# The start of a fused decoder layer: which queue brings x, in which pieces the first weights are split, and fewer filler products

## The reference

```python
z = h @ w_in[l]          # h is x: (256, 2048); w_in: (2048, 1024 + 512 + 512 + 64 + 4096)
u_ssm, c_q, c_kv, k_rope_raw, gate_logits = jnp.split(z, split_at, axis=-1)
```

## Time and profile before

| | |
|---|---|
| time, median of 3 runs | 1333.01 us (1332.86 to 1333.1) |
| profiled execution | 1332.76 us, of which the span from first to last instruction is 1330.6 us |
| PE busy | 1320.0 us, 99% of the span |
| DVE busy, ACT busy | 835.4 us (63%), 648.7 us (49%) |
| transfers | 253.21 MB, mean 190 GB/s |

### The profile page before, as it was taken

The page is one execution under the profiler, slowest core; times in us unless marked ns, Lnnn a source line. Parts: engine busy times, 40 slices in busy tenths (PEclk is TensorE's granted clock), DMA queues, the critical chain, the costliest instruction groups (busy, mean ns, idle before and its releaser), DMA issues.

```text
span 1330.6 us, 28260 instructions
## 1 busy us (share of the span) xinstructions
PE 1320.0 (99%) x11052; PEld 1249.1 (94%) x11052; DVE 835.4 (63%) x1232; ACT 648.7 (49%) x910; POOL 23.1 (2%) x50
## 2 busy tenths in 40 slices
PE   9999999999999999999999999999999999999998
PEld 8999999999999998879999999999999998888896
DVE  6787868687786776577555655555555555545545
ACT  5566556474656454365444444444444453434332
POOL 0022000000001000000000000000000000000000
PEclk9999999999999999999999999999999999999999
DMA  8656545545476775754656666666666676556562
GB/s 287 206 190 191 161 157 159 154 141 183 135 192 184 250 246 197 241 169 149 200 190 190 191 195 194 191 190 197 195 190 192 215 236 193 191 173 216 175 207 98
DMA packets 79774, 253.21 MB, mean 190 GB/s; under 512 B 16544, under 2 KB 17504, under 8 KB 79584
## 3 DMA queue, kind: packets, MB, share of 16 engines
q1 hardware_dynamic: 78304, 251.69, 59.8%
q0 software_dynamic: 1408, 0.63, 0.2%
HBM read 248.08 MB, written 2.10 MB: 188 GB/s over the span
## 4 chain that ended last, share of the span: by engine, by line
PE 96%; DVE 2%; ACT 1%; DMA 1%; issue 0%; SPq 0%; DVEq 0%
PE ps L895 22%; PE ps L896 22%; PE ps L897 22%; PE ps L907 9%; PE ps L908 9%; PE ps L909 9%; PE ps L1103 1%; DVE wlo L477 1%; PE ps L1122 1%; PE ps L1099 1%; DMA xrow<-x 0%; PE ps L1034 0%; PE ps L1075 0%; PE ps L1048 0%; PE ps L1056 0%; DVE sqsum L1484 0%
## 5 line engine op out<-in xcount | busy, mean ns | idle before, releaser
L477 DVE TENSOR_TENSOR wlo<-raw,whi 128x1024 fp32r<-128x1024 f32 x450 | 546.8, 1223 | 334.1 <-ACT whi L521 332.1
L521 ACT ACTIVATE whi<-raw 128x1024 fp32r<-128x1024 f32 x450 | 476.6, 1061 | 543.0 <-PE ps L897 340.1
L895 PE MATMUL ps<-hT,whi 128*128 128x256 f32 x1376 | 378.4, 275 | 0.0
L896 PE MATMUL ps<-hT,whi 128*128 128x256 f32 x1376 | 378.4, 275 | 0.0
L897 PE MATMUL ps<-hT,wlo 128*128 128x256 f32 x1376 | 378.4, 275 | 0.0
L895 PEld LDWEIGHTS ps<-hT,whi 128*128 128x128 f32 x1376 | 258.3, 188 | 0.0
L896 PEld LDWEIGHTS ps<-hT,whi 128*128 128x128 f32 x1376 | 258.3, 188 | 0.0
L897 PEld LDWEIGHTS ps<-hT,wlo 128*128 128x128 f32 x1376 | 258.3, 188 | 0.0
L895 PE MATMUL ps<-xT,whi 128*128 128x256 f32 x784 | 221.6, 283 | 0.8 <-DVE wlo L477 0.7
L897 PE MATMUL ps<-xT,wlo 128*128 128x256 f32 x784 | 216.4, 276 | 0.0
L896 PE MATMUL ps<-xT,whi 128*128 128x256 f32 x784 | 216.3, 276 | 0.0
(11 more groups left out here) (274 smaller groups left out, 1482.3 us busy)
## 6 DMA issues: line engine op xcount, KB each, us to landing
raw<-slabs SPq DMA_DIRECT2D x450, 512.0 KB, 4.2
xrow<-x SPq DMA_DIRECT2D x4, 512.0 KB, 6.8
rows<-x SPq DMA_DIRECT2D x4, 512.0 KB, 6.1
gb<-ln_rows SPq DMA_DIRECT2D x4, 512.0 KB, 7.1
eraw<-slabs SPq DMA_DIRECT2D x4, 512.0 KB, 6.3
gb<-ln_rows SPq DMA_DIRECT2D x1, 2048.0 KB, 8.6
out<-rows SPq DMA_DIRECT2D x8, 256.0 KB, 2.6
yb<-u SPq DMA_DIRECT2D x32, 24.0 KB, 3.1
```

Source lines behind the costliest of these rows:

```text
L477: unit.tensor_tensor(wlo[:, s, :], raw[:, s, :], whi[:, s, :].bitcast(F32), ALU.subtract).then_inc(done, 1 + empty_after)
L521: nc.scalar.activation(whi[:, s, :], raw[:, s, :], ACT.Copy).then_inc(hi_ready, 1 + empty + first)
L895: mm(ps[:, bank, 0:TOK], hi, src[:, kt, 0, :], start=(first and n == 0), stop=False)
L896: mm(ps[:, bank, 0:TOK], hi, src[:, kt, 1, :], start=False, stop=False)
```

## The change

Three things are edited, all in the first 19 us.

1. x1, the second quarter of x, is issued by ACT as its first instruction, on ACT's own transfer queue. On SP the order becomes identity, x0, first slab (v = 2), x2, x3, second slab (v = 3), v = 4, v = 5.
2. The high and low parts of the first slab are made in two halves of 512 columns (`first_high`, `first_low`, with the new semaphores `first_hi` and `first_lo`). PE starts the first four tiles when the first half is there, and waits for the second before the last four.
3. `warm(5)` becomes `warm(4)` and `warm(6)` becomes `warm(4)`.

```diff
             sy.dma_start(cst[:, 0:P], consts[:, 0:P]).then_inc(in_ident, 16)
             load_x(0)
-            load_x(1)
             first_slab(0, 2)
-            first_slab(2, 3)
             load_x(2)
             load_x(3)
+            first_slab(2, 3)
...
+            def first_high():
+
+                ac.wait_ge(raw_ready[FRONT0], 16)
+                for c in range(2):
+                    cut = slice(c * 512, c * 512 + 512)
+                    ins = nc.scalar.activation(whi[:, FRONT0, cut], raw[:, FRONT0, cut], ACT.Copy)
+                    if c == 0:
+                        ins.then_inc(first_hi, 1)
+                    else:
+                        ins.then_inc(hi_ready, 1 + FRONT0)
+
+            ac.dma_start(xrow[:, 1, 0:SLAB], x.rearrange("(t p) d -> p t d", p=P)[:, 1, 0:SLAB]).then_inc(in_x[1], 16)
             for k in range(8):
                 ac.wait_ge(xt_psum, k + 1)
                 nc.scalar.activation(xT[:, 2 * k:2 * k + 2, 0, :],
                                      ps[:, 2 + k % 6, :].rearrange("p (a t) -> p a t", a=2), ACT.Copy).then_inc(xt_hi, 1)
-                if k in (1, 3):
-                    high(0, FRONT0, FRONT_PER, k // 2)
+                if k == 1:
+                    first_high()
+                if k == 3:
+                    high(0, FRONT0, FRONT_PER, 1)
...
             pe.wait_ge(warm_ready, 1)
-            warm(5)
+            warm(4)
             pe.wait_ge(in_ident, 16)
             for t in range(2):
                 for k in range(4):
                     turn_x(k, t)
-            warm(6)
+            warm(4)
 
 
             pe.wait_ge(xt_lo, 2)
-            pe.wait_ge(lo_dve, FRONT0 + 1)
+            pe.wait_ge(first_lo, 1)
             fold_tile(0, FRONT0, 0, xT, range(0, 4), True, False)
...
             pe.wait_ge(xt_lo, 4)
+            pe.wait_ge(lo_dve, FRONT0 + 1)
             fold_tile(0, FRONT0, 4, xT, range(4, 8), False, False).then_inc(slab_used, 1 + FRONT0)
...
+            def first_low():
+
+                for c in range(2):
+                    cut = slice(c * 512, c * 512 + 512)
+                    if c == 0:
+                        ve.wait_ge(first_hi, 1)
+                    else:
+                        ve.wait_ge(hi_ready, FRONT0 + 1)
+                    ins = V.tensor_tensor(wlo[:, FRONT0, cut], raw[:, FRONT0, cut], whi[:, FRONT0, cut].bitcast(F32), ALU.subtract)
+                    if c == 0:
+                        ins.then_inc(first_lo, 1)
+                    else:
+                        ins.then_inc(lo_dve, 1 + FRONT0)
```

More of the change, by code:

```diff
@@ L242, in build @@
         hi_ready, lo_dve, slab_used = sem("hi_ready"), sem("lo_dve"), sem("slab_used")
+        first_hi, first_lo = sem("first_hi"), sem("first_lo")
         early_ready = [sem(f"early_ready{n}") for n in range(EARLY)]
@@ L471, in _, with low_part @@
             sy.wait_ge(out_stored, 8 * 16)
-        def low_part(eng, unit, v, s, done, empty_after=0):
+        def low_part(eng, unit, v, s, done):
             eng.wait_ge(hi_ready, v + 1)
             unit.tensor_tensor(wlo[:, s, :], raw[:, s, :], whi[:, s, :].bitcast(F32), ALU.subtract
-                               ).then_inc(done, 1 + empty_after)
+                               ).then_inc(done, 1)
         @block.gpsimd
@@ L519, in high @@
                     empty += 1
-                first = FRONT0 if isinstance(i, int) and i == 0 and start + k == FRONT0 else 0
-                nc.scalar.activation(whi[:, s, :], raw[:, s, :], ACT.Copy).then_inc(hi_ready, 1 + empty + first)
+                nc.scalar.activation(whi[:, s, :], raw[:, s, :], ACT.Copy).then_inc(hi_ready, 1 + empty)
+            def first_high():
[8 more added lines that the diff above has]
+            ac.dma_start(xrow[:, 1, 0:SLAB], x.rearrange("(t p) d -> p t d", p=P)[:, 1, 0:SLAB]).then_inc(in_x[1], 16)
             for k in range(8):
@@ L1343, in front_low @@
                 v = n + FRONT0
-                low_part(ve, V, v, v % RING, lo_dve, FRONT0 if n == 0 else 0)
+                low_part(ve, V, v, v % RING, lo_dve)
+            def first_low():
[10 more added lines that the diff above has]
+                        ins.then_inc(lo_dve, 1 + FRONT0)
             V.memset(prob[:], 0.0).then_inc(warm_ready, 1)
@@ L1350, in _ @@
                                 xT[:, 2 * k:2 * k + 2, 0, :].bitcast(F32), ALU.subtract).then_inc(xt_lo, 1)
-                if k in (1, 3):
-                    front_low(k // 2)
+                if k == 1:
+                    first_low()
+                if k == 3:
+                    front_low(1)
             re, im, dt = sp[:, 0, :], sp[:, 1, :], sp[:, 2, :]
```

## The result

The changed kernel takes 1334.86 us (median of 22, 1334.02 to 1335.7), the kernel before 1333.06 (22, 1332.36 to 1333.76): ratio 1.0012, 95% interval 1.0007 to 1.0018. It is 1.8 us slower, clear of noise and inside the 0.2% that the prediction called no change. The forecast was 1332.6 with a range to 1334.4; the time lies outside. It is almost the number of the rival "the clock stays low" (1334.7, chance 0.23). The profiled execution took 1335.62, the second longest of the 22, with a span of 1333.4.

A forecast was written before the change was run, and what follows sets the result against it. PE's work bounds the kernel (busy 1320.0 of 1330.6 us). Halves' 0.87 less x0's later landing leaves 0.44: 1332.76 - 0.44 = 1332.3 profiled, median 1332.6; range 1331.9 to 1334.4.

The forecast's parts named there:

- the clock stays low: Rival: PE's clock not up when x0 lands, transposes 0.22 us apart; +1.7 us, 1334.7, chance 0.23.
- Part 3: Forecast step on transfer queues: x1 on ACT's queue only changes order; x0 lands at 6.7, giving back about half the halves' gain.
- X0: Time x0 lands at the start of the kernel: taken as 6.7, against 5.3 before.
- K: Start of ACT's first `xT`: 7.63 before, forecast 8.06.
- S: Start of PE's first real product: 11.20 before, forecast 10.76, 0.44 us earlier.
- the halves: First slab's parts made 512 wide: first product 2.7 us after first `xT` instead of 3.57, worth 0.87 us.
- The way from the first product to v = 4: PE's stretch from first real product to v = 4: 7.82 us, claimed to stay, so v = 4 starts at 18.6.
- the cap: Second slab's landing limits the gain at v = 4 to roughly 0.7 us (start 18.3) if S falls under about 10.4.
- Fewer zero products: Filler before and after the transposes: the later cut worth 0.4 us, only because of the halves; the earlier filler ends at 5.1.
- From 19.02 on nothing later: From the start of v = 4 no wait for weights is listed, so its shift moves the end by as much.
- the 0.44: Forecast gain in us at the first real product, carried to v = 4 and to the end.
- equal turns: Two queues sharing the transfer engines alike: x0 would land with x1, near 6.8.

## Why the prediction was wrong

**The step that failed is x0's landing.** Part 3 took X0 = 6.7, with bounds 5.3 and 7.15, because both quarters are asked for within 0.45 us. Measured are 7.4 to 7.8 in the six profiles with x1 on ACT. The upper bound failed too, by 0.2 to 0.6: I had counted the bytes of x0 and x1, set the earlier request to x0's credit, and put the identity ahead of x0 on SP at nothing. The packets show what it did: with ACT's queue at work beside it, it took 3.7 us to land instead of 1.9, and x0's own packets began at 4.37 instead of 2.26. By then 111 of ACT's 144 packets had started. The rest of the engines' work up to 7.55 was not x0's alone: SP's queue had started 1.04 MB, of which identity and x0 are 0.59. Whether the identity is the whole reason or ACT's earlier request a part of it stays open; no run separates them.

**With X0 went the choice among the rivals.** The sum K = X0 + 1.36 was right (7.55 gives 8.91 at the high clock; measured 9.20 in the kernel with 9 products, whose filler holds the transposes to 0.3 after x0). At X0 = 7.55 the gap behind the filler is 2.6 us, not the 1.6 that I had weighed, and both profiles of the changed kernel show the low clock through all 16 transposes and most of the zero products. The rival's arithmetic held: S = X0 + 7.0 less the rise, 13.7 measured; +1.7 forecast, +1.8 measured. That the two are so near is partly luck: the rival was priced with x0 at 6.7, and part of the 1.8 is x0's landing at 7.6. Its chance of 0.23 was too small, and the range, cut at 1334.4, left out just its centre. The filler ended in the earlier trace rows where the rise came; that should have weighed more, and more still had I known that the rise in the same kernel can come at 6.9.

**How the 1.8 us divide.** With 9 products the first `xT` is 1.57 later (9.20 against 7.63), of which some 0.2 is the filler; the halves give back 0.91 at the first product: 0.66 in the profiles, 0.60 in the medians. The rest is the clock: 1.97 between the two profiles (21.68 - 19.71), but the changed kernel's is a long execution; 1.2 between their medians, 0.7 when the second median of the changed kernel is taken. That the clock has a part is shown: nothing but the filler differs. The landing's part is seen in the profiles, and in the time only without the halves (1.5 us, of which some 0.5 is the filler). That the clock's is the larger is likely, and its size is not known to better than some 0.5 us.

**What held.** The halves: 2.66 or 2.67 from first `xT` to first product in all six profiles where neither filler nor slab is late, for 2.7 forecast. The way from the first product to v = 4: 7.85 in the kernel with 9 products, 7.82 before; 7.96 in the changed kernel, and 8.29 where the second slab's landing is the cap. One issue less on SP brought nothing. ACT's issue cost nothing. Fewer zero products cost nothing while x0 comes in time (1333.01 against 1332.83, inside the interval). Nothing was seen to be added around the span: 2.2 us, as before.

**What held only by halves.** "From 19.02 on nothing later": losses did pass to the end (+2.66 at v = 4, +2.8 in the span), gains unevenly (0.25 at v = 4 and nothing at v = 8 with x1 on SP; 0.62 and 0.23 with the quarters swapped; 0.48 and 0.54 with 5 products and `xT` 4 and 5 moved; all in single profiles). I checked v = 6, which has room, and not v = 8, which has next to none. Whether the 0.44 would have come with x0 in time the runs do not settle: the kernel with all but the queue measured 0.0, the one with the quarters swapped 0.43 less, and either interval holds both.

## What to carry to other kernels

On full transfer engines a second queue made nothing faster here; it reordered. Put on it what is needed first, and let the consumer take the pieces in the order in which they land. Count what stands ahead on the other queue in packets, not only in bytes: 64 KB in 512-byte packets went ahead of x0 here, and x0 began 2 us later.

A filler that is to bring the clock up is sized by the wait that it covers: whatever makes the awaited transfer later must lengthen it, and a shorter filler before a later transfer pays twice. What it runs over the landing is lost as well (some 0.2 and 0.5 us with 9 products here).

An early gain is worth what the chain with least room behind it lets through; look for every later wait that begins at the moved event, not only the next one.

## What the runs showed of the hardware

With x on two queues, the 512 KB on ACT's landed 1.7 to 2.5 us ahead of the 512 KB on SP's, in nine profiles, and not in the near tie that I took equal turns to mean. ACT's was asked for 0.45 us earlier and SP's stood behind the identity. The Trainium skill ("DMA: Bandwidth & Descriptors", "Issuing engines are not separate DMA queues") says that the transfers of both share the engines and interleave, and the rows agree: from 3.0 to 4.0 us each queue started 45 packets. Since these were 4096 bytes on one and 512 on the other, the interleaving did not bring the two quarters in together.

The clock's rise, by the starts of single PE instructions, with what PE did before it. At work without a gap from 1.33 to the rise: 5.3 and 6.9 (kernel before, twice), 4.3 and 6.5 (halves alone, 6 and 4 products behind), 6.6 and 6.9 (9 products), 6.6 (5 products, x0 on ACT), 4.5 (4 products, x0 on ACT). With a gap behind the filler: by 5.6, inside the gap (three kernels with 4 products, gap 0.35 to 0.45), 7.4 (4 products, gap 0.6), 8.2 (1 product, 2.8), 10.4 (5 products, 1.6), 13.2 and 13.0 (4 products, 2.6 and 2.8). At 7.4 it cost next to nothing, because x1 was only there at 7.3. The Trainium skill, "TensorE: Matmul & The Clock Gate", Part 1, says that the moment of the rise varies from run to run. The two profiles of the kernel before agree, 1.6 us apart with one program; the two of the changed kernel, with nearly one moment, do not show it. The two groups of times 1 to 1.5 us apart (`warm(1)`, and x1 on ACT alone) would fit it, but only one execution of each has a profile.
